# Work on the fifth tile of the next block between the two norms of a decoder trunk, in place of filler matmuls

## The chip, the cores and the metric

The kernel runs on one core of a Trainium2 chip. The metric is the device time of one execution in microseconds; the kernel before takes 794.01 us, the median of three runs (793.81 to 794.09).

## The reference

Two layers on 272 tokens (16 learned meta tokens and 256 of the sequence) of 1024 features, all in float32. Each layer is (cut):

```python
h = rms_norm(r, norm_mix_pre)
proj = h @ w_in        # q and kv latents, rotary key, diff q/k/v, two gates
...                    # latent attention and differential attention
mix = (sigmoid(g_a) * out_a + sigmoid(g_b) * out_b) @ w_out
r = r + rms_norm(mix, norm_mix_post)
h = rms_norm(r, norm_ffn_pre)
gu = h @ w_gate_up
ff = (silu(gu[..., :D_FF]) * gu[..., D_FF:]) @ w_down
r = r + rms_norm(ff, norm_ffn_post)
```

`rms_norm(x, gain)` is x / sqrt(mean(x*x) + 1e-6) * gain over all 1024 features. The result is r of the 256 tokens after layer 2.

## The kernel before

Features lie on the partitions and tokens on the free axis: r, y (the output of a block before its norm) and the block input h are 8 chunks of 128 features x 272 tokens; from the middle of layer 1 on only 256 tokens are needed. A float32 product is made of three matmuls in the rounded format float32r: each operand is split into a high and a low part, and w_hi·h_hi, w_hi·h_lo and w_lo·h_hi are added in PSUM (`block`, L1330 to L1332). A tile is 128 output features: 8 chunks x 3 matmuls for an input of 1024 features.

Weights come by DMA, 128x1024 at a time, to w_raw (4 buffers). ScalarE copies each to w_hi (L438) and VectorE subtracts to get w_lo (L883); both rings have 8 slots, and the splits run 6 to 7 slots ahead of TensorE. Each engine has its own written order of work; semaphores join them (`slot_ready` waits for a w_lo, `bank_free` and `emptied` for the evacuation of the tile that had the PSUM bank before, `pe_done` for a finished tile). VectorE empties the tiles in order and counts them in tile_free.

The three boundaries b = 1, 2, 3 are mix to gate/up in layer 0, down to the latents of layer 1, and mix to gate/up in layer 1. At each the block's last tile is squared, the squares (summed by GpSimd in acc) are summed over the features by TensorE (`norm_sums`, L1423), ScalarE takes the root (L485), VectorE the reciprocal (L891), and TensorE spreads it by transposes (`norm_spread`, L1442) into bank 7. VectorE then makes y·gain·rstd (L915) and adds it to r (L927) chunk by chunk, ScalarE makes h_hi (L492) and the next squares (L451), VectorE h_lo (L905). The norm of the next block isn't applied to h; its root is applied when its tiles are emptied (`rstd_h`), so its sums and spread stand inside the tiles that follow. Between its own norm steps TensorE multiplies an identity matrix into bank 6, 10 and 28 times (`keep_clock`, L1449, called by `post_norm`).

Then `first_tiles` (L1355, L1364) makes the first four tiles of the next block side by side, chunk by chunk, as h_hi and h_lo come. The fifth tile ("tile 4": `gu4`, or `lat 4` in layer 1) follows alone, with `norm_sums` of the next norm in front of chunk 0; in gate/up `norm_spread` stands in front of its chunk 4, in the latents it stands in `dq 1` in front of chunk 2. Gate/up tiles 0 to 5 use banks 0 to 5; tile 6 uses bank 2 again (it waits for the evacuation of tile 2), tile 7 bank 3, tile 8 bank 0, tile 9 bank 1, tile 10 bank 2. In gate/up VectorE copies rstd_h out of bank 7 (`take`, L896) and then goes pair by pair: evacuate (L1260), split (L883), evacuate, split, with the low part of the product (L1274) between. In the latents of layer 1, ScalarE squares and copies tile i (L451, L476), VectorE makes its low part (L974), with a split by each engine between; behind latent 4 come ScalarE's root (L485) and VectorE's reciprocal (L891).

During the gates of layer 0 VectorE computes the factors lambda (`lambdas`, L1000 to L1005), then the softmax of the meta tokens' rows (L1162 to L1175), whose result TensorE transposes inside gate tile 4 (`meta_transposes`, L1564).

Of the kernel before, what the change touches and what calls it, by code (L numbers as in the profile page):

```python
# [23 lines left out]
P = 128  # L24
D_MODEL, SEQ, DEPTH, N_META = 1024, 256, 2, 16
TOK = SEQ + N_META
# [17 lines left out]

TAIL = 8
# [141 lines left out]
def build_trunk(nc: bass.Bass, xT, x_rows, first_weights, weights, lam_in, consts, gain_rows, out):  # L187
# [4 lines left out]
    with ctx:  # L192
# [3 lines left out]
        def place(at, tensors):  # L196
# [16 lines left out]
            ("small", [P, 80], f32), ("pm_room", [P, 2, TOK], f32),  # L213
# [41 lines left out]

        (gain_bc, r_tok), _ = place(_, [("gain_bc", [P, D_MODEL], f32), ("r_tok", [P, 2, D_MODEL], f32)])
        assert _ <= nc.sbuf_usable_end
# [22 lines left out]
        gsub = small[:, 72:74]  # L280
        pscale, nscale = small[:, 32:35], small[:, 36:38]
# [25 lines left out]
        r_ready, h_hi, h_lo = sem("r_ready"), sem("h_hi_ready"), sem("h_lo_ready")  # L307
        lat_ready_hi = sem("lat_hi_ready")
# [55 lines left out]


        @block.sync
        def _(sp):
            def load(n, width, i=None, per=0):

                m = n if i is None else n + per * i  # L370
                if n >= FIRST + RAW:

                    sp.wait_ge(lo_ready, m - RAW + 1)
                src = weights[bass.ds(m * P, P), 0:width] if i is not None else weights[m * P:(m + 1) * P, 0:width]
                sp.dma_start(w_raw[:, n % RAW, 0:width], src).then_inc(raw_in[n % RAW], 16)


            for i, (a, b) in enumerate(PIECES):
# [33 lines left out]
            sp.wait_ge(pe_done, plan.tile_done[plan.tile[DEPTH - 1, "out", KC - 1]])  # L412
# [10 lines left out]
        def _(act):  # L423
# [44 lines left out]
            def latent(l, i):  # L468

                c0 = T0(l) if i < QC else 0  # L470
                t, K = plan.tile[l, "lat", i], NORMS * l + (NQ if i < QC else NKV)
                act.wait_ge(pe_done, plan.tile_done[t])
                if l and i == 0:
                    act.wait_ge(pt_ready, UNITS * l)
                square(K, i if i < QC else i - QC, ps[bank_of(t)][:, c0:TOK], c0)
                act.activation(lat_hi[:, i, c0:], ps[bank_of(t)][:, c0:TOK], ACT.Copy,  # L476
                               scale=gain[:, l, G_Q + i:G_Q + i + 1]).then_inc(lat_ready_hi, 1)
# [65 lines left out]
            for l in range(DEPTH):  # L543
# [194 lines left out]
                if l < DEPTH - 1:  # L738
                    for m in range(KC):
                        for j in range(4):  # L740
                            split(SD + 4 * m + j + HI_AHEAD)
                        square_tile(K0 + POST_FFN, TD + m, m)
                    root(K0 + POST_FFN, 7, D_MODEL, t0)
                    boundary(2 * l + 2, K0 + NORMS + PRE_MIX, G_MIXPRE, l + 1)
# [116 lines left out]
        def _(dve):  # L861
# [46 lines left out]
            def residual(b, K, gp, lp, t0):  # L908
# [3 lines left out]
                def product(c):  # L912
# [4 lines left out]
                    if c < KC - 1:  # L917
                        made[c] = step(ins)
                    else:
                        ins.then_inc(norm_ready, 1)  # L920

                def add(c):
                    if c < KC - 1:
                        after(made[c])
                    else:
                        dve.wait_ge(norm_ready, K + 1)
                    dve.tensor_tensor(r[:, c, t0:], r[:, c, t0:], parts[c % 2][:, t0:], ALU.add).then_inc(r_ready, 1)  # L927
# [9 lines left out]
                lo_part(b, KC - 2, *nxt(b), t0)  # L937
                lo_part(b, KC - 1, *nxt(b), t0)

            def nxt(b):  # L940
                return (G_FFNPRE, b // 2) if b % 2 else (G_MIXPRE, b // 2)
# [27 lines left out]
            def latent_lo(l, i):  # L969

                c0 = T0(l) if i < QC else 0
                t = plan.tile[l, "lat", i]
                dve.wait_ge(lat_ready_hi, 5 * l + i + 1)
                dve.scalar_tensor_tensor(out=lat_lo[:, i, c0:], in0=ps[bank_of(t)][:, c0:TOK], scalar=gain[:, l, G_Q + i:G_Q + i + 1],  # L974
# [21 lines left out]
            def lambdas():  # L996

                dve.wait_ge(lam_exp, 1)
                for l in range(DEPTH):
# [3 lines left out]
                    step(dve.tensor_scalar(gsub[:, l:l + 1], gain[:, l, G_SUB:G_SUB + 1], 1.0 - LAM_INIT[l], None, ALU.mult))  # L1003
                after(steps[0])
                dve.memset(idle, 0.0).then_inc(const_ready, 1)  # L1005

            for l in range(DEPTH):
# [239 lines left out]
                def pair(j, i=None, first=False):  # L1247
# [7 lines left out]
                    for k, buf in ((0, gbuf), (1, ubuf)):  # L1255
# [4 lines left out]
                        dve.tensor_tensor(buf[:, j % 2, t0:], ps[bank_of(t + k + (0 if i is None else RING))][:, t0:TOK], rstd_h[:, t0:], ALU.mult).then_inc(tile_free, 1)  # L1260
# [24 lines left out]
                if l < DEPTH - 1:  # L1285
                    for m in range(KC):
                        for j in range(4):
                            split(S("down") + 4 * m + j + AHEAD)
                        to_y(K0 + POST_FFN, TL("down") + m, m)
                    recip(K0 + POST_FFN, t0)  # L1290
# [25 lines left out]
        def _(pe):  # L1316
# [17 lines left out]
            def tile(t, n, at, width, src, t0, i=None, per=0, inside=None):  # L1334

                bank_free(t, i, per)
                for k, (a, b) in enumerate(src):
                    if inside and k in inside:
                        inside[k]()
                    mm = block(t, n, at + k * width, width, a, b, t0, k == 0, k == len(src) - 1, ahead=0 if i is None else per)  # L1340
                mm.then_inc(pe_done, 1)

# [121 lines left out]
            for l in range(DEPTH):  # L1464
# [13 lines left out]
                tile(TL("lat") + 4, S("lat") + 4, 0, P, full, 0, inside={0: lambda: norm_sums(K0 + PRE_MIX, 7, 0)} if l else None)  # L1478
# [231 lines left out]
                post_norm(K0 + POST_MIX)  # L1710
# [3 lines left out]
                for j in range(4, 4 + RING):  # L1714
                    slot_ready(g0 + j)
                    tile(gt + j, g0 + j, 0, P, late, t0, inside={0: lambda: norm_sums(K0 + PRE_FFN, 7, t0), 4: lambda: norm_spread(K0 + PRE_FFN, 7, t0)} if j == 4 else None)
# [20 lines left out]
                post_norm(K0 + POST_FFN)  # L1737
# [149 lines left out]
```

## Time and profile before

| | |
|---|---|
| median of three runs | 794.01 us |
| the profiled execution | 794.08 us |
| its span | 792.3 us |
| granted TensorE clock | 0.999 |
| TensorE busy | 785.0 us (99%), 6268 matmuls |
| VectorE busy | 572.3 us (72%) |
| ScalarE busy | 451.7 us (57%) |
| GpSimd busy | 138.6 us (17%) |
| bytes moved | 134.87 MB, mean 170 GB/s |

The span goes from the first to the last instruction that the profiler shows; the execution is 1.8 us longer. Busy of TensorE is an upper bound of its use, because matmuls are pipelined: one of 128x272 is shown with 0.29 us while the next starts 0.13 us later. PE is the matmul row, PEld the weight loads that overlap it. An idle time stands in brackets with the engine and the tensor that ended it. "issue" is idle time for which the profile shows no releaser.

### The profile page before, as it was taken

To read this page: it belongs to the slowest core of one execution; us is meant where nothing else is said; L and a number is where in the kernel's file an instruction comes from. 1 tells how busy PE (TensorE), PEld (TensorE's weight loads), DVE (VectorE), ACT (ScalarE), POOL (GpSimd) and SP (SyncE) were. 2 spreads that over 40 slices of the span, in tenths; PEclk is the share of its full clock that TensorE was granted. 3 is DMA by queue.
4 is the path that set the end of the run, shared out by engine and by line. 5 is a ranking of instruction groups with operands and counts; after the bars stand their busy time and mean duration, and the time that the engine had idled before them with its cause. 6 is when DMAs were issued, how large, how long until landed. Compare 5 with 4: busy or idle time off the path is not lost.

```text
span 792.3 us, 16792 instructions
## 1 busy us (share of the span) xinstructions
PE 785.0 (99%) x6268; PEld 762.2 (96%) x6268; DVE 572.3 (72%) x996; ACT 451.7 (57%) x766; POOL 138.6 (17%) x150
## 2 busy tenths in 40 slices
PE   9999999999999999999999999999999999999997
PEld 9999899999999999999999999999999999999885
DVE  6899787696787666766668987967866977676432
ACT  6657665675475454455557467656755755454331
POOL 0312000233321111101123302001433211111000
PEclk9999999999999999999999999999999999999999
DMA  9767433355166565355654674334552776667971
GB/s 334 255 225 241 131 109 107 107 187 160 55 206 218 161 176 172 115 166 170 198 173 134 192 241 153 107 108 132 187 167 73 227 215 178 195 175 193 276 135 54
DMA packets 55531, 134.87 MB, mean 170 GB/s; under 512 B 20896, under 2 KB 21536, under 8 KB 55344
## 3 DMA queue, kind: packets, MB, share of 16 engines
q1 hardware_dynamic: 38608, 131.43, 52.9%
q10 hardware_dynamic: 16864, 2.62, 2.0%
q8 instruction: 41, 0.67, 0.3%
q14 instruction: 18, 0.15, 0.1%
HBM read 131.93 MB, written 2.10 MB: 169 GB/s over the span
## 4 chain that ended last, share of the span: by engine, by line
PE 97%; DVE 1%; ACT 1%; issue 0%; DVEq 0%
PE bank L1330 24%; PE bank L1332 24%; PE bank L1331 24%; PE bank L1364 4%; PE bank L1748 3%; PE bank L1749 3%; PE bank L1747 3%; PE bank L1355 2%; PE bank L1602 2%; PE bank L1574 2%; PE bank L1621 1%; PE bank L1449 1%; PE bank L1423 1%; PE bank L1576 1%; PE bank L1380 1%; PE bank L1391 1%
## 5 line engine op out<-in xcount | busy, mean ns | idle before, releaser
L883 DVE TENSOR_TENSOR w_lo<-w_raw,w_hi 128x1024 fp32r<-128x1024 f32 x246 | 330.9, 1348 | 37.4 <-ACT w_hi L438 34.5
L1330 PE MATMUL bank<-h_hi,w_hi 128*128 128x272 f32 (+1 forms) x1200 | 346.0, 288 | 0.0
L1332 PE MATMUL bank<-h_hi,w_lo 128*128 128x272 f32 (+1 forms) x1200 | 342.8, 286 | 0.0
L1331 PE MATMUL bank<-h_lo,w_hi 128*128 128x272 f32 (+1 forms) x1200 | 341.9, 285 | 0.0
L438 ACT ACTIVATE w_hi<-w_raw 128x1024 fp32r<-128x1024 f32 x246 | 258.5, 1054 | 122.1 <-PE bank L1332 57.0
L1330 PEld LDWEIGHTS bank<-h_hi,w_hi 128*128 128x128 f32 x1200 | 226.2, 188 | 0.7
L1332 PEld LDWEIGHTS bank<-h_hi,w_lo 128*128 128x128 f32 x1200 | 226.2, 188 | 0.0
L1331 PEld LDWEIGHTS bank<-h_lo,w_hi 128*128 128x128 f32 x1200 | 226.0, 188 | 0.0
L848 POOL TENSOR_TENSOR pbuf<-sbuf,ubuf 128x272 f32<-128x272 f32 (+1 forms) x44 | 38.5, 874 | 205.6 <-DVE ubuf L1260 204.0
L779 POOL TENSOR_TENSOR acc<-acc,sq 128x272 f32<-128x272 f32 (+1 forms) x45 | 47.3, 1052 | 137.2 <-ACT sq L451 137.0
L1260 DVE TENSOR_TENSOR ubuf<-bank,rstd_h 128x272 f32<-128x272 f32 (+1 forms) x44 | 18.9, 430 | 44.9 <-PE bank L1332 44.9
L1330 PE MATMUL bank<-ff_hi,w_hi 128*128 128x272 f32 x176 | 50.7, 288 | 0.0
L1331 PE MATMUL bank<-ff_lo,w_hi 128*128 128x272 f32 x176 | 50.7, 288 | 0.0
L1332 PE MATMUL bank<-ff_hi,w_lo 128*128 128x272 f32 x176 | 50.5, 287 | 0.0
L721 ACT ACTIVATE sbuf<-gbuf 128x272 f32<-128x272 f32 (+1 forms) x44 | 18.7, 425 | 52.3 <-DVE gbuf L1260 52.2
L596 ACT ACTIVATE e_t<-e_t,small 128x272 f32<-128x272 f32 (+1 forms) x48 | 22.1, 462 | 44.9 <-DVE small L1115 44.9
L1748 PE MATMUL bank<-w_lo,ff_hi 128*128 128x512 f32 x88 | 34.7, 395 | 0.0
L1749 PE MATMUL bank<-w_hi,ff_lo 128*128 128x512 f32 x88 | 34.7, 394 | 0.0
L1747 PE MATMUL bank<-w_hi,ff_hi 128*128 128x512 f32 x88 | 34.6, 393 | 0.0
L1234 DVE COPY y<-bank 128x272 f32<-128x272 f32 (+1 forms) x24 | 10.4, 435 | 31.5 <-PE bank L1332 20.1
L1332 PEld LDWEIGHTS bank<-ff_hi,w_lo 128*128 128x128 f32 x176 | 33.1, 188 | 0.0
L1330 PEld LDWEIGHTS bank<-ff_hi,w_hi 128*128 128x128 f32 x176 | 33.1, 188 | 0.0
(238 smaller groups left out, 1229.2 us busy)
## 6 DMA issues: line engine op xcount, KB each, us to landing
w_raw<-weights SPq DMA_DIRECT2D x216, 512.0 KB, 3.9
w_raw<-weights SPq DMA_DIRECT2D x16, 384.0 KB, 3.2
w_raw<-weights SPq DMA_DIRECT2D x16, 320.0 KB, 2.9
w_first<-first_weights SPq DMA_DIRECT2D x2, 512.0 KB, 7.5
x_tok<-x_rows SPq DMA_DIRECT2D x1, 1024.0 KB, 11.0
turn<-y ACTq DMA_DIRECT2D x4, 256.0 KB, 7.1
r_tok<-turn ACTq DMA_DIRECT2D x8, 128.0 KB, 6.3
out_tokens<-o_tok SPq DMA_DIRECT2D x4, 256.0 KB, 2.0
```

The costliest lines, as they stand in the source:

```text
L438: act.activation(w_hi[:, n % RING, :], w_raw[:, n % RAW, :], ACT.Copy).then_inc(hi_ready, 1)
L596: last = act.activation(e[:, a:b], e[:, a:b], ACT.Exp, bias=mx[u % 2][:, s + part:s + part + 1], scale=-1.0, accum_out=sm[u % 2][:, s + pa ...
L779: pool.tensor_tensor(acc[:, K % 2, t0:], acc[:, K % 2, t0:], sq[:, plan.sq_place[K, c], t0:], ALU.add).then_inc(sq_added, 1)
L848: pool.tensor_tensor(pbuf[:, j % 2, t0:], sbuf_[:, j % 2, t0:], ubuf[:, j % 2, t0:], ALU.mult).then_inc(ff_prod, 1)
L883: dve.tensor_tensor(w_lo[:, n % RING, :], w_raw[:, n % RAW, :], w_hi[:, n % RING, :].bitcast(f32), ALU.subtract).then_inc(lo_ready, 1)
L1330: pe.matmul(dst, wh, hi, start=first, stop=False)
L1331: pe.matmul(dst, wh, lo, start=False, stop=False)
L1332: return pe.matmul(dst, wl, hi, start=False, stop=last)
L1364: pe.matmul(ps[bank_of(t)][:, t0:TOK], w[:, n % RING, k * P:(k + 1) * P], src[k][0], start=k == 0 and q == 0, stop=False)
L1747: pe.matmul(dst, x_hi, wh, start=k == 0, stop=False)
L1748: pe.matmul(dst, x_hi, wl, start=False, stop=False)
L1749: return pe.matmul(dst, x_lo, wh, start=False, stop=k == FC - 1)
```

## The change

At a boundary the next block's tile 4 is split by linearity. Its input is h = (r_old + y·g_post·rstd)·g_next, so w·h = w·(r_old·g_next) + rstd·[w·(y·g_post·g_next)]. For the first three of eight chunks (EARLY = 3) ScalarE and VectorE make high and low parts of r_old·g_next (old_hi, old_lo) and y·g_post·g_next (new_hi, new_lo) during the last tiles of the block, one part per tile. `post_norm` loses its fillers: TensorE multiplies the old parts into tile 4's bank and the new parts into bank 6. ScalarE copies bank 6 to new_part, VectorE multiplies that by the spread rstd, and when tile 4's other five chunks are done, VectorE adds tile and new_part; what read the tile's bank before now reads new_part. Nine products of two gains are made in `lambdas`. The sums of the next norm stand in front of chunk 3 of tile 4, the spread (gate/up) in front of chunk 7. The load of gain_bc, whose place overlaps new_part, waits for tile gu4 of the last layer instead of the last out tile. The diff, cut:

```diff
+EARLY = 3
...
 ScalarE
@@ latent(l, i)
+                src = ps[bank_of(t)][:, c0:TOK]
+                if l and i == 4:
+                    act.wait_ge(early_sum, 2 * l)
+                    src = new_part[:, c0:]
+                else:
+                    act.wait_ge(pe_done, plan.tile_done[t])
...
+            def early_high(b, i):
+                src, factor, hi, _ = early_chunk(b, i)
+                if b == 1 and i == EARLY:
+                    act.wait_ge(gains_ready, 1)
+                act.activation(hi, src, ACT.Copy, scale=factor).then_inc(early_hi, 1)
@@ boundary(b, K, g, l)
                 for c in range(KC):
+                    if c == 2:
+                        act.wait_ge(new_product, b)
+                        act.activation(new_part[:, t0:], ps[6][:, t0:TOK], ACT.Copy).then_inc(new_copied, 1)
@@ out tiles (down tiles of layer 0 likewise, with b = 2 l + 2)
                     square_tile(K0 + POST_MIX, TL("out") + m, m)
+                    if m < 2 * EARLY:
+                        early_high(2 * l + 1, m)
 VectorE
@@ residual(b, K, gp, lp, t0)
                 lo_part(b, KC - 2, *nxt(b), t0)
+                dve.wait_ge(new_copied, b)
+                dve.tensor_tensor(new_part[:, t0:], new_part[:, t0:], ps[7][:, 64 + t0:64 + TOK], ALU.mult).then_inc(norm_ready, 1)
                 lo_part(b, KC - 1, *nxt(b), t0)
...
+            def early_low(b, i):
+                src, factor, hi, lo = early_chunk(b, i)
+                dve.wait_ge(early_hi, 2 * EARLY * (b - 1) + i + 1)
+                dve.scalar_tensor_tensor(out=lo, in0=src, scalar=factor, in1=hi.bitcast(f32), op0=ALU.mult, op1=ALU.subtract).then_inc(early_lo, 1)
+            def early_tile(b, t):
+                t0 = boundary_from(b)
+                dve.wait_ge(pe_done, plan.tile_done[t])
+                dve.wait_ge(norm_ready, NORMS * ((b - 1) // 2) + (POST_MIX if b % 2 else POST_FFN) + 1)
+                dve.tensor_tensor(new_part[:, t0:], ps[bank_of(t)][:, t0:TOK], new_part[:, t0:], ALU.add).then_inc(early_sum, 1)
+                dve.wait_ge(early_sum, b)
@@ latent_lo(l, i)
+                if l and i == 4:
+                    early_tile(2 * l, t)
+                    src = new_part[:, c0:]
                 dve.wait_ge(lat_ready_hi, 5 * l + i + 1)
@@ lambdas()
+                for b in range(1, 2 * DEPTH):
+                    for c in range(EARLY):
+                        step(dve.tensor_tensor(both_gains[EARLY * (b - 1) + c], gain_before(b, c), gain_behind(b, c), ALU.mult))
                 after(steps[0])
@@ out tiles (down tiles likewise)
                     to_y(K0 + POST_MIX, TL("out") + m, m)
+                    if 1 <= m <= 2 * EARLY:
+                        early_low(2 * l + 1, m - 1)
@@ pair(j, i, first), gate/up
+                        if j == 2 and k == 0 and i is None:
+                            early_tile(2 * l + 1, t)
+                            src = new_part[:, t0:]
 TensorE
+            def early_old(t, n, c, t0):
+                dst = ps[bank_of(t)][:, t0:TOK]
+                wh, wl = (w[:, n % RING, c * P:(c + 1) * P] for w in (w_hi, w_lo))
+                pe.matmul(dst, wh, old_hi[:, c, t0:], start=c == 0, stop=False)
+                pe.matmul(dst, wl, old_hi[:, c, t0:], start=False, stop=False)
+                pe.matmul(dst, wh, old_lo[:, c, t0:], start=False, stop=False)
...
@@ post_norm
-            def post_norm(K):
+            def post_norm(K, b, t, n):
                 norm_sums(K, 7, t0)
-                keep_clock(10)
+                pe.wait_ge(early_lo, 2 * EARLY * b)
+                slot_ready(n)
+                bank_free(t)
+                early_old(t, n, 0, t0)
                 norm_spread(K, 7, t0)
-                keep_clock(28)
+                for c in range(1, EARLY):
+                    early_old(t, n, c, t0)
+                for c in range(EARLY):
+                    mm = early_new(n, c, t0)
+                mm.then_inc(new_product, 1)
@@ tile 4 of the latents of layer 1, and of gate/up
-                tile(TL("lat") + 4, S("lat") + 4, 0, P, full, 0, inside={0: lambda: norm_sums(K0 + PRE_MIX, 7, 0)} if l else None)
+                tile(TL("lat") + 4, S("lat") + 4, 0, P, full, 0, inside={EARLY: lambda: norm_sums(K0 + PRE_MIX, 7, 0)} if l else None, done=EARLY if l else 0)
...
+                        tile(gt + j, g0 + j, 0, P, late, t0, inside={EARLY: lambda: norm_sums(K0 + PRE_FFN, 7, t0), 7: lambda: norm_spread(K0 + PRE_FFN, 7, t0)}, done=EARLY)
```

`early_new` is `early_old` with new_hi, new_lo and bank 6. `tile(..., done=3)` skips the first three chunks and the wait for the bank.

## Rows read from the trace of the kernel before

**Rows 1.** The page, part 1: busy us (share of the span) and instructions of each engine.

```profile
PE 785.0 (99%) x6268; PEld 762.2 (96%) x6268; DVE 572.3 (72%) x996; ACT 451.7 (57%) x766; POOL 138.6 (17%) x150
```

**Rows 2.** Timeline, first boundary: start us, us, engine, line, operation, count, idle before.

```profile
203.70 0.30 PEld L1442 LDWEIGHTS bank<-cst,small 128*128 128x128 f32 x3 [0.16 <-DVE small L891]
...
203.97 1.66 PEld L1449 LDWEIGHTS bank<-identb 128*128 128x128 bf16 x28
...
205.29 0.52 ACT L492 ACTIVATE h_hi<-x_sb 128x272 fp32r<-128x272 f32 x1 [1.85 <-DVE x_sb L927]
...
205.92 0.19 PEld L1364 LDWEIGHTS bank<-h_hi,w_hi 128*128 128x128 f32 x1 [0.29 <-issue]
```

**Rows 3.** Timeline of PE in and behind tile gu4 of layer 0.

```profile
220.29 0.49 PE L1442 MATMUL bank<-cst,small 128*128 128x128 f32 x3
220.53 0.37 PE L1330 MATMUL bank<-h_hi,w_hi 128*128 128x272 f32 x1
...
220.99 0.29 PE L1330 MATMUL bank<-h_hi,w_hi 128*128 128x272 f32 x1
...
225.16 0.29 PE L1330 MATMUL bank<-h_hi,w_hi 128*128 128x272 f32 x1
```

**Rows 4.** Timeline of DVE behind the spread in gate/up of layer 0.

```profile
220.81 0.44 DVE L896 COPY rstd_h<-bank 128x272 f32<-128x272 f32 x1 [1.48 <-PE bank L1442]
...
224.32 0.43 DVE L1260 TENSOR_TENSOR gbuf<-bank,rstd_h 128x272 f32<-128x272 f32 x1
...
226.05 0.43 DVE L1260 TENSOR_TENSOR ubuf<-bank,rstd_h 128x272 f32<-128x272 f32 x1
```

**Rows 5.** Timeline around the start of tile gu6 of layer 1.

```profile
617.00 0.42 DVE L1260 TENSOR_TENSOR gbuf<-bank,rstd_h 128x256 f32<-128x256 f32 x1
...
617.33 0.19 PEld L1332 LDWEIGHTS bank<-h_hi,w_lo 128*128 128x128 f32 x1
...
617.53 0.19 PEld L1330 LDWEIGHTS bank<-h_hi,w_hi 128*128 128x128 f32 x1
```

**Rows 6.** Timeline of latent tile 4 of layer 1, until the spread.

```profile
427.94 1.21 DVE L883 TENSOR_TENSOR w_lo<-w_raw,w_hi 128x1024 fp32r<-128x1024 f32 x1
...
428.88 0.38 ACT L451 ACTIVATE sq<-bank 128x272 f32<-128x272 f32 x1
...
429.53 0.27 ACT L485 ACTIVATE small<-bank,small 128x3 f32<-128x3 f32 x1
...
429.68 0.50 DVE L974 SCALAR_TENSOR_TENSOR lat_lo<-bank,x_sb,lat_hi 128x272 fp32r<-128x272 f32 x1 [0.53 <-ACT lat_hi L476]
...
430.09 0.17 DVE L891 RECIPROCAL small<-small 128x3 f32<-128x3 f32 x1
...
431.15 0.34 PEld L1442 LDWEIGHTS bank<-cst,small 128*128 128x128 f32 x3
```

**Rows 7.** Timeline: lambdas and the next place at which DVE waits for PE, and PEld.

```profile
87.91 0.15 DVE L1002 TENSOR_SCALAR small<-small 128x1 f32<-128x1 f32 x1
87.98 0.14 DVE L1003 TENSOR_SCALAR small<-x_sb 128x1 f32<-128x1 f32 x1
88.04 0.15 DVE L1000 TENSOR_TENSOR small<-small 128x1 f32<-128x1 f32 x1
...
93.17 0.41 PEld L1564 LDWEIGHTS bank<-cst,pm 16*16 16x16 f32 x14 [0.30 <-DVE pm L1175]
...
106.84 0.44 DVE L901 TENSOR_TENSOR gates<-bank,rstd_h 128x272 f32<-128x272 f32 x1 [0.23 <-PE bank L1332]
```

**Rows 8.** Timeline: DVE at tile out 6 of layer 0; PEld at the third boundary's sums.

```profile
198.83 0.44 DVE L1234 COPY y<-bank 128x272 f32<-128x272 f32 x1 [1.46 <-PE bank L1332]
...
596.64 0.52 PEld L1423 LDWEIGHTS bank<-small,sq 128*128 128x128 f32 x4 [0.22 <-ACT sq L451]
```

**Rows 9.** Timeline of DVE: the reciprocal behind the first tiles, layer 0.

```profile
219.16 0.18 DVE L891 RECIPROCAL small<-small 128x3 f32<-128x3 f32 x1 [2.35 <-ACT small L485]
```

**Rows 10.** Windows, first boundary: busy us (PE, PEld, DVE, ACT, POOL), granted clock, DMA share, GB/s.

```profile
201.50:206.00 4.50, 4.35 (x57) 4.03 (x55) 2.27 (x6) 1.37 (x4) 0.00 (x0) 1.00 0.31 118
```

More of the change, by code:

```diff
@@ L212, in build_trunk @@
             ("cst", [P, C_ALL - 512 + 128], f32), ("identb", [P, P], bf16), ("maskb", [P, P], bf16),
-            ("small", [P, 80], f32), ("pm_room", [P, 2, TOK], f32),
+            ("small", [P, 88], f32), ("pm_room", [P, 2, TOK], f32),
             ("tres", [P, TOK], f32)])
@@ L254, in build_trunk @@
             ("ubuf", [P, 2, TOK], f32), ("sbuf", [P, 2, TOK], f32), ("pbuf", [P, 2, TOK], f32)])
+        (old_hi, old_lo, new_hi, new_lo, new_part), _end = place(att0 + 4 * 2 * FC * TOK, [
+            ("old_hi", [P, EARLY, TOK], f32r), ("old_lo", [P, EARLY, TOK], f32r), ("new_hi", [P, EARLY, TOK], f32r),
+            ("new_lo", [P, EARLY, TOK], f32r), ("new_part", [P, TOK], f32)])
         (gain_bc, r_tok), _ = place(_, [("gain_bc", [P, D_MODEL], f32), ("r_tok", [P, 2, D_MODEL], f32)])
-        assert _ <= nc.sbuf_usable_end
+        assert max(_, _end) <= nc.sbuf_usable_end
         (o_tok, o_sq), _ = place(base + 4 * ((RAW + 2 * RING) * SLOT + GAIN_COLS + KC * TOK), [("o_tok", [P, 2, D_MODEL], f32), ("o_sq", [P, 2, D_MODEL], f32)])
@@ L280, in build_trunk @@
         gsub = small[:, 72:74]
+        both_gains = [small[:, i:i + 1] for i in (*range(80, 88), 38)]
         pscale, nscale = small[:, 32:35], small[:, 36:38]
@@ L307, in build_trunk @@
         r_ready, h_hi, h_lo = sem("r_ready"), sem("h_hi_ready"), sem("h_lo_ready")
+        early_hi, early_lo, gains_ready, new_product, new_copied, early_sum = (
+            sem(n) for n in ("early_hi_ready", "early_lo_ready", "gains_ready", "new_product", "new_copied", "early_sum"))
         lat_ready_hi = sem("lat_hi_ready")
@@ L363, in boundary_from, with nxt, gain_before, gain_behind @@
             return N_META if b >= 2 * DEPTH - 1 else 0
+        def nxt(b):
+            return (G_FFNPRE, b // 2) if b % 2 else (G_MIXPRE, b // 2)
+        def gain_before(b, c):
+            l, g = (b - 1) // 2, G_MIXPOST if b % 2 else G_FFNPOST
+            return gain[:, l, g + c:g + c + 1]
+        def gain_behind(b, c):
+            g, l = nxt(b)
+            return gain[:, l, g + c:g + c + 1]
+        def early_chunk(b, i):
+            t0, c = boundary_from(b), i % EARLY
+            if i < EARLY:
+                return r[:, c, t0:], gain_behind(b, c), old_hi[:, c, t0:], old_lo[:, c, t0:]
+            return y[:, c, t0:], both_gains[EARLY * (b - 1) + c], new_hi[:, c, t0:], new_lo[:, c, t0:]
         @block.sync
@@ L410, in _ @@
                     first = d0 + 4 * KC
-            sp.wait_ge(pe_done, plan.tile_done[plan.tile[DEPTH - 1, "out", KC - 1]])
+            sp.wait_ge(pe_done, plan.tile_done[plan.tile[DEPTH - 1, "gu", 4]])
             sp.dma_start(gain_bc[:, :], gain_rows).then_inc(gain_rows_in, 16)
@@ L471, in latent @@
                 t, K = plan.tile[l, "lat", i], NORMS * l + (NQ if i < QC else NKV)
-                act.wait_ge(pe_done, plan.tile_done[t])
+                src = ps[bank_of(t)][:, c0:TOK]
[4 more added lines that the diff above has]
+                    act.wait_ge(pe_done, plan.tile_done[t])
                 if l and i == 0:
                     act.wait_ge(pt_ready, UNITS * l)
-                square(K, i if i < QC else i - QC, ps[bank_of(t)][:, c0:TOK], c0)
-                act.activation(lat_hi[:, i, c0:], ps[bank_of(t)][:, c0:TOK], ACT.Copy,
+                square(K, i if i < QC else i - QC, src, c0)
+                act.activation(lat_hi[:, i, c0:], src, ACT.Copy,
                                scale=gain[:, l, G_Q + i:G_Q + i + 1]).then_inc(lat_ready_hi, 1)
@@ L742, in _ @@
                         square_tile(K0 + POST_FFN, TD + m, m)
+                        if m < 2 * EARLY:
+                            early_high(2 * l + 2, m)
                     root(K0 + POST_FFN, 7, D_MODEL, t0)
@@ L916, in product @@
                                                    in1=ps[7][:, 64 + t0:64 + TOK], op0=ALU.mult, op1=ALU.mult)
[L917 to L920, printed above, removed]
+                    made[c] = step(ins)
                 def add(c):
[L923 to L926, printed above, removed]
+                    after(made[c])
                     dve.tensor_tensor(r[:, c, t0:], r[:, c, t0:], parts[c % 2][:, t0:], ALU.add).then_inc(r_ready, 1)
@@ L972, in latent_lo @@
                 t = plan.tile[l, "lat", i]
+                src = ps[bank_of(t)][:, c0:TOK]
+                if l and i == 4:
+                    early_tile(2 * l, t)
+                    src = new_part[:, c0:]
                 dve.wait_ge(lat_ready_hi, 5 * l + i + 1)
-                dve.scalar_tensor_tensor(out=lat_lo[:, i, c0:], in0=ps[bank_of(t)][:, c0:TOK], scalar=gain[:, l, G_Q + i:G_Q + i + 1],
+                dve.scalar_tensor_tensor(out=lat_lo[:, i, c0:], in0=src, scalar=gain[:, l, G_Q + i:G_Q + i + 1],
                                          in1=lat_hi[:, i, c0:].bitcast(f32), op0=ALU.mult, op1=ALU.subtract).then_inc(tile_free, 1)
@@ L1332, in block, with tile @@
                 return pe.matmul(dst, wl, hi, start=False, stop=last)
-            def tile(t, n, at, width, src, t0, i=None, per=0, inside=None):
-                bank_free(t, i, per)
+            def tile(t, n, at, width, src, t0, i=None, per=0, inside=None, done=0):
+                if not done:
+                    bank_free(t, i, per)
                 for k, (a, b) in enumerate(src):
+                    if k < done:
+                        continue
                     if inside and k in inside:
@@ L1341, in tile, with early_new @@
                 mm.then_inc(pe_done, 1)
+            def early_old(t, n, c, t0):
[4 more added lines that the diff above has]
+                pe.matmul(dst, wh, old_lo[:, c, t0:], start=False, stop=False)
+            def early_new(n, c, t0):
+                dst = ps[6][:, t0:TOK]
+                wh, wl = (w[:, n % RING, c * P:(c + 1) * P] for w in (w_hi, w_lo))
+                pe.matmul(dst, wh, new_hi[:, c, t0:], start=c == 0, stop=False)
+                pe.matmul(dst, wl, new_hi[:, c, t0:], start=False, stop=False)
+                return pe.matmul(dst, wh, new_lo[:, c, t0:], start=False, stop=c == EARLY - 1)
             def first_tiles(tiles, ready):
@@ L1715, in _ @@
                     slot_ready(g0 + j)
-                    tile(gt + j, g0 + j, 0, P, late, t0, inside={0: lambda: norm_sums(K0 + PRE_FFN, 7, t0), 4: lambda: norm_spread(K0 + PRE_FFN, 7, t0)} if j == 4 else None)
+                    if j == 4:
+                        tile(gt + j, g0 + j, 0, P, late, t0, inside={EARLY: lambda: norm_sums(K0 + PRE_FFN, 7, t0), 7: lambda: norm_spread(K0 + PRE_FFN, 7, t0)}, done=EARLY)
+                    else:
+                        tile(gt + j, g0 + j, 0, P, late, t0)
                 with pe.Fori(1, 5) as i:
@@ L1736, in _ @@
                         mm.then_inc(pe_done, 1)
-                post_norm(K0 + POST_FFN)
+                post_norm(K0 + POST_FFN, 2 * l + 2, plan.tile[l + 1, "lat", 4], plan.slot[l + 1, "lat", 4])
             d0 = S("down")
```

11 lines of the change are left out of this document (6 added, 5 removed).

## Prediction

> **What bounds the kernel now.** I read the page first: TensorE is busy 785.0 of 792.3 us, VectorE 72%, ScalarE 57% [rows 1]. Time can only be won by giving TensorE fewer real matmuls, or by filling a place where it does nothing of use. The chain of waits names such places: three times it leaves TensorE for the norm between two blocks. The timeline of the first one shows what happens there: the transposes that spread the reciprocal root load at 203.70, then 28 filler matmuls load from 203.97 for 1.66 us, VectorE and ScalarE make the first h_hi (to 205.81), and the first real weight load comes at 205.92 [rows 2]. So the fillers cover a latency of two other engines; TensorE arrives 0.29 us early. The change puts real work of the tile "number 4" of the next block there. Whether that is time won is decided by what TensorE meets next, so I followed each boundary on until TensorE next needs something from VectorE, and looked at the idle notes of PEld (a real stall shows there) and at VectorE's order.
>
> **The window itself.** In place of 28 fillers stand 2 old chunks and 3 new ones, 15 matmuls; the first old chunk (3) replaces the 10 fillers before the spread. A matmul of 128x272 takes its turn every 0.126 us: 33 of them lie between 220.99 and 225.16 [rows 3]. 15 x 0.126 = 1.90 us from 203.97 is 205.87, just in front of 205.92. The first ones behind transposes cost a little more: three in 0.46 us instead of 0.38 [rows 3]. So the first tiles begin 0 to 0.1 us later at each boundary; below nothing isn't possible, since they wait for the h_hi whose chain (sums, root, reciprocal, spread, product, add) isn't touched. I take 0.05 in all, bounds 0 to 0.3.
>
> **What leaves tile 4.** Nine matmuls, at each of three boundaries: 9 x 0.126 = 1.14 us, about 3.4 us in all (the third has 256 columns, so a little less). This is the gain if nothing else is late. At each boundary something is.
>
> *First boundary (gate/up, layer 0).* The sums now stand in front of chunk 3 and the spread in front of chunk 7: again 12 matmuls lie between them, so the spread stays at 220.29 and VectorE's copy of it at 220.81 [rows 3, 4]. From there VectorE runs without a pause: evacuate gu0, split, gu1, split, gu2 at 224.32 to 224.75 [rows 4]. Tile gu6 writes bank 2, which gu2 held. Before, TensorE came to gu6 at 225.16, 0.41 us after the bank was free. Now it arrives at 225.16 - 1.14 = 224.02 and waits for 224.75, plus 0.11 us from release to weight load (the third boundary shows such a restart: copy over at 617.42, load at 617.53 [rows 5]). It takes up at 224.86 instead of 225.16. The restart loses some overlap, so I take 0.2 us won, bounds 0.1 and 0.35. gu7 needs gu3, free at 226.48 [rows 4], and starts near 227.9: no second wait. VectorE's extra addition at gu4, 0.44 us by the row of an evacuation [rows 4], falls where it is behind but TensorE doesn't need it: the next bank from that queue is gu6's, four tiles on.
>
> *Third boundary (gate/up, layer 1).* Same order, but here TensorE already waits for that bank before the change: the weight load of gu6 comes at 617.53, 0.20 us after the one before it at 617.33, and gu2's evacuation ends at 617.42 [rows 5]. Arriving 1.1 us earlier wins nothing. I take 0, bounds 0 and 0.1.
>
> *Second boundary (latents of layer 1).* No bank is short, but the spread in dq1 waits for the reciprocal, and in front of that stand ScalarE's and VectorE's work on latent tile 4. Before: VectorE ends a split at 429.15, ScalarE squares at 428.88 and roots at 429.53, VectorE makes the low part at 429.68 and the reciprocal at 430.09 to 430.26; the spread loads at 431.15 [rows 6], so it has nearly a microsecond to spare. After: VectorE must first add new_part (0.44 us, as an evacuation), about 429.1 to 429.55, and only then can ScalarE square, 0.7 us later than before. Root, low part and reciprocal move with it, the reciprocal to about 430.95. TensorE comes to the spread at 431.15 - 1.14 = 430.01 and waits until about 431.0. Won: 0.15 us, bounds 0 and 0.5 (0.5 if the addition came a split earlier).
>
> **The setup.** lambdas() gets nine more multiplications of 128x1 and the end of the previous one is waited for. They stand in the middle of a VectorE run that TensorE waits for: it idles 0.30 us in front of meta_transposes until VectorE's pm, and VectorE has no wait for TensorE again until 106.84 [rows 7]. No cover there. Independent ones of these start 0.06 to 0.07 us apart (87.91, 87.98, 88.04 [rows 7]): 9 x 0.065 = 0.6 us, all of it on the path. From above: if each took its whole 0.15 us, 1.4 us; from below 0.5. I take 0.6, since the new ones are independent like the rows'. The Trainium skill, "VectorE: DVE Perf Modes", section Terms, says that a flush follows every operation and the next can't issue until the pipe is empty. By that the nine cost 1.4 us and the sum rises by 0.8; the trace disagrees, with starts 0.07 us apart for operations 0.15 us long.
>
> **The stages in front of the boundary.** ScalarE gets six copies (0.52 us each by h_hi's row [rows 2]) and VectorE six low parts (0.50 us [rows 6]), one a tile. VectorE idles 1.46 us in such a tile [rows 8], so both fit. Nearest to the edge is the third boundary: ScalarE's table load stands behind the sixth copy, the square of tile 6 and POOL's addition come about 0.4 us later and end near 595.9, where the first sums begin; but the second sums wait for the last square anyway, 0.22 us idle [rows 8]. Cost 0, bounds 0 and 0.1. During the first tiles VectorE's multiplication of new_part (0.44) meets an idle time of 2.35 us in front of the next reciprocal [rows 9]. On TensorE itself 18 matmuls in the window (3 in front of the spread, 15 behind) replace 9 in tile 4 and the 38 fillers.
>
> **Sum.** Span: + 0.6 (setup) + 0.05 (window) - 0.2 - 0.15 - 0 = + 0.3 us. The profiled run had 794.08 us, so 794.4; from the median, 794.01, it is 794.3. 0.2% of it is 1.6 us, about what a measurement of this kernel can tell from no change.
>
> **Rivals.**
> A. The nine matmuls are won at each boundary: - 3.4 + 0.6 = - 2.8, 791.2 us. For it: TensorE is 99% busy, and it does 27 matmuls fewer outside the windows. Against it: the bank of gu2 and the reciprocal, both with times that TensorE's arrival doesn't move. It would need VectorE to free gu2 by 224.0. Chance 0.08.
> B. Part of it: one of the two waits is shorter than I read, worth 0.6 to 1.1 us at one boundary, with the setup 0.6: 793.2 to 793.8 us; two of them make 792.4. Chance 0.1, nearly all within 0.2%.
> C. Slower: with the fillers gone, the pauses cost TensorE its clock. The place is the first tiles and gu6 (0.3 us before the spread, then about 0.85 us; also 1.0 us in dq1). The granted clock is 1.00 in the first boundary's stretch, where the longest pause is 0.29 us [rows 2, 10]; no pause of 1 us is there to read. At the level below, 1.2 GHz, a matmul takes its turn in 0.25 us, so each tile of 24 costs 3.0 us more. It decides from 11 matmuls at that level (1.4 us); one tile gives 797.3 us. The Trainium skill, "TensorE: Matmul & The Clock Gate", Part 1, has throttled as the default and activity as what releases it; by that rule the longer pauses are a risk and the dense real matmuls in the window none. Chance 0.04.
> D. The small operations cost their whole duration, or the window overruns at each boundary: 795.1 to 795.5 us. Chance 0.08, a fifth of it beyond 0.2% with the other bounds.
> My forecast holds 0.7. From these: faster by over 0.2% 0.09, within 0.85, slower 0.06. The range for eight in ten is 793.2 to 795.3: the bounds of the terms, and B and D at their near ends.
>
> **What would show it.** The profile after should have PEld idle of about 0.85 us at gu6 of layer 0, released by VectorE's gbuf, and about 1.0 us at gu6 of layer 1; an idle time of about 0.9 us at the spread in dq1, released by the reciprocal; 0.9 instead of 0.30 us in front of meta_transposes; first weight loads of the next block with 0.1 us or less idle; and no filler between 6 us and the end. The forecast is wrong if gu6 starts without idle time, if the gap between the reciprocal and the spread stays as wide as before in dq1, if the nine small operations cost nothing to the 93 us mark, or if the granted clock falls below 1.0 after a pause.

## The result, and the profile after

The changed kernel takes 795.3 us (median of 22 runs, 794.9 to 795.68) beside 794.03 us (22 runs, 793.64 to 794.71) of the kernel before on the same chip: a ratio of 1.0014, interval 1.0008 to 1.0020. That is within 0.2%, a little slower, and 1.0 us above the 794.3 forecast: the median lies on the upper bound of the range, 795.3. The profiled execution has a span of 793.8 us (792.3 before).

The page after, part 1 (busy us, share of the span, instructions of each engine):

```profile
PE 783.6 (99%) x6181; PEld 760.2 (96%) x6181; DVE 582.3 (73%) x1029; ACT 459.2 (58%) x787; POOL 143.1 (18%) x150
```

TensorE has 1.4 us less busy time than in [rows 1], and the span is 1.5 us longer: it now waits. The list of PEld's waits says where (line waited for: us in total, times, longest):

```profile
PEld bank L1528 <- DVE small L936: 2.1, 4, 1.2
PEld bank L1397 <- DVE w_lo L928: 2.0, 2, 1.1
PEld bank L1535 <- DVE identb L998: 1.1, 1, 1.1
PEld bank L1657 <- DVE pm L1234: 0.9, 1, 0.9
```

The third one stands before the first real matmul and was there before. The first was 0.3 us in all; it now has the 0.3 us in front of each boundary's spread and one wait of 1.16 us in dq1. The second is new, the fourth has grown. Now place by place; I line the two traces up by their matmuls and give TensorE's "offset", the start of a matmul after minus the start of the same one before. It is +0.3 us ahead of the setup.

*Setup.* VectorE's nine multiplications, and the load of `meta_transposes` behind them on PEld:

```profile
88.67 0.70 DVE L1062 TENSOR_TENSOR small<-x_sb 128x1 f32<-128x1 f32 x9
94.11 0.66 PEld L1657 LDWEIGHTS bank<-cst,pm 16*16 16x16 f32 x24 [0.95 <-DVE pm L1234]
```

Nine in 0.70 us from the first start to the last end, so some 0.07 us from start to start. The load comes at 94.11 and not 93.17 [rows 7], its idle time is 0.95 instead of 0.30, and the offset goes from 0.32 to 0.94.

*First boundary.* PEld, from the last sums to the first tiles:

```profile
203.84 0.19 PEld L1417 LDWEIGHTS bank<-old_hi,w_hi 128*128 128x128 f32 x1
...
204.57 0.30 PEld L1528 LDWEIGHTS bank<-cst,small 128*128 128x128 f32 x3 [0.30 <-DVE small L936]
204.84 0.19 PEld L1417 LDWEIGHTS bank<-old_hi,w_hi 128*128 128x128 f32 x1
...
206.58 0.19 PEld L1427 LDWEIGHTS bank<-new_lo,w_hi 128*128 128x128 f32 x1
206.80 0.19 PEld L1450 LDWEIGHTS bank<-h_hi,w_hi 128*128 128x128 f32 x1
```

Real matmuls stand where [rows 2] has fillers, and the first tile's load at 206.80 is the 205.92 of before plus the offset of 0.88: nothing won and nothing lost.

*gate/up tile gu6, layer 0.* VectorE's evacuation of gu2, then PEld and the first matmul:

```profile
225.18 0.43 DVE L1325 TENSOR_TENSOR gbuf<-bank,rstd_h 128x272 f32<-128x272 f32 x1
```

```profile
224.62 0.19 PEld L1399 LDWEIGHTS bank<-h_hi,w_lo 128*128 128x128 f32 x1
225.73 0.19 PEld L1397 LDWEIGHTS bank<-h_hi,w_hi 128*128 128x128 f32 x1 [0.92 <-DVE w_lo L928]
225.76 0.37 PE L1397 MATMUL bank<-h_hi,w_hi 128*128 128x272 f32 x1 [0.72 <-DVE gbuf L1325]
```

TensorE arrives 1.13 us sooner and then waits 0.92 us. Less the offset of 0.88, the evacuation starts at 224.30 [rows 4: 224.32] and the load at 224.85. The offset falls to 0.68: 0.2 us won. The two rows of this start disagree on the releaser: the load's names the split w_lo, the matmul's the evacuation, gbuf. The times speak for the evacuation: the load comes 0.12 us after its end at 225.61, while the next w_lo runs on to 226.96; experiment a_bank6 settles it.

*dq1, layer 1.* VectorE, then ScalarE, then PEld:

```profile
428.86 1.21 DVE L928 TENSOR_TENSOR w_lo<-w_raw,w_hi 128x1024 fp32r<-128x1024 f32 x1
430.00 0.43 DVE L992 TENSOR_TENSOR new_part<-bank,new_part 128x272 f32<-128x272 f32 x1
431.40 0.62 DVE L1030 SCALAR_TENSOR_TENSOR lat_lo<-new_part,x_sb,lat_hi 128x272 fp32r<-128x272 f32 x1 [0.98 <-ACT lat_hi L507]
431.94 0.16 DVE L936 RECIPROCAL small<-small 128x3 f32<-128x3 f32 x1
```

```profile
430.46 0.43 ACT L477 ACTIVATE sq<-new_part 128x272 f32<-128x272 f32 x1 [0.42 <-DVE new_part L992]
430.79 0.51 ACT L507 ACTIVATE lat_hi<-new_part,x_sb 128x272 fp32r<-128x272 f32 x1
431.20 0.24 ACT L516 ACTIVATE small<-bank,small 128x3 f32<-128x3 f32 x1
```

```profile
432.16 0.30 PEld L1528 LDWEIGHTS bank<-cst,small 128*128 128x128 f32 x3 [1.16 <-DVE small L936]
```

All of it hangs on the addition (new_part), which stands behind a split: square, high part, root, low part, reciprocal, in a row. TensorE had 9 matmuls fewer and waits 1.16 us. The offset is 0.94 ahead of tile 4 and 0.91 to 0.96 behind the spread: nothing won.

*gu6, layer 1.* VectorE's evacuation of gu2, and PEld:

```profile
618.17 0.42 DVE L1325 TENSOR_TENSOR gbuf<-bank,rstd_h 128x256 f32<-128x256 f32 x1
618.70 0.19 PEld L1397 LDWEIGHTS bank<-h_hi,w_hi 128*128 128x128 f32 x1 [1.07 <-DVE w_lo L928]
```

The load comes 0.11 us after the evacuation's end. 618.70 less the offset of 1.17 is 617.53, the same time as in [rows 5]. Nothing won.

*Between these places* the offset should stand still, and it does not. It falls by under 0.1 us over the attention of layer 0 and grows by 0.26 us over the 128x272 matmuls of the down projection of layer 0, by 0.2 over the attention and out tiles of layer 1, by 0.34 over the last stage. The first and the last 128x512 matmul of that last stage (264 of them), before and after:

```profile
725.53 0.40 PE L1747 MATMUL bank<-w_hi,ff_hi 128*128 128x512 f32 x1
...
786.48 0.39 PE L1749 MATMUL bank<-w_hi,ff_lo 128*128 128x512 f32 x1
```

```profile
726.71 0.40 PE L1843 MATMUL bank<-w_hi,ff_hi 128*128 128x512 f32 x1
...
787.99 0.40 PE L1845 MATMUL bank<-w_hi,ff_lo 128*128 128x512 f32 x1
```

60.95 us before and 61.28 after, with not one wait in it: every matmul takes its turn 1.3 ns later (0.2330 against 0.2318 us). No step of the prediction has this. The granted clock is 1.00 in all the stretches looked at, here at the first boundary and around the three long waits behind it (columns: us, PE busy, clock, DMA share, GB/s):

```profile
203.00:207.00 4.00, 3.92 (x31) 1.00 0.35 123
220.00:226.00 6.00, 5.28 (x43) 1.00 0.33 98
428.00:433.00 5.00, 4.04 (x35) 1.00 0.83 285
616.00:620.00 4.00, 3.10 (x27) 1.00 0.48 131
```

### The profile page after: what moved, and what is told of

Same layout as the page of the kernel before. It is cut to its first block, busy times and chain, and to the rows that moved or that the text cites. A ratio compares the mean times of both kernels' runs of the same rounds, so it can differ in the third digit from the quotient of the medians.

```text
span 793.8 us, 16676 instructions
## 1 busy us (share of the span) xinstructions
PE 783.6 (99%) x6181; PEld 760.2 (96%) x6181; DVE 582.3 (73%) x1029; ACT 459.2 (58%) x787; POOL 143.1 (18%) x150
## 4 chain that ended last, share of the span: by engine, by line
PE 95%; DVE 3%; ACT 1%; issue 1%; DVEq 0%; ACTq 0%
PE bank L1397 24%; PE bank L1398 23%; PE bank L1399 23%; PE bank L1450 4%; PE bank L1843 3%; PE bank L1845 3%; PE bank L1844 3%; PE bank L1441 2%; PE bank L1695 2%; PE bank L1667 2%; DVE w_lo L928 1%; PE bank L1714 1%; PE bank L1509 1%; PE bank L1669 1%; PE bank L1535 1%
## 5 line engine op out<-in xcount | busy, mean ns | idle before, releaser
L1397 PE MATMUL bank<-h_hi,w_hi 128*128 128x272 f32 (+1 forms) x1191 | 343.0, 288 | 1.6 <-DVE gbuf L1325 1.6
L1397 PEld LDWEIGHTS bank<-h_hi,w_hi 128*128 128x128 f32 x1191 | 224.6, 189 | 2.7 <-DVE w_lo L928 2.0
L824 POOL TENSOR_TENSOR acc<-acc,sq 128x272 f32<-128x272 f32 (+1 forms) x45 | 53.2, 1183 | 131.8 <-ACT sq L477 131.6
L1397 PE MATMUL bank<-ff_hi,w_hi 128*128 128x272 f32 x176 | 50.7, 288 | 0.0
L1397 PEld LDWEIGHTS bank<-ff_hi,w_hi 128*128 128x128 f32 x176 | 33.2, 188 | 0.0
L1398 PEld LDWEIGHTS bank<-ff_lo,w_hi 128*128 128x128 f32 x176 | 33.2, 188 | 0.0
```

Of the source, the lines that this page charges most:

```text
L824: pool.tensor_tensor(acc[:, K % 2, t0:], acc[:, K % 2, t0:], sq[:, plan.sq_place[K, c], t0:], ALU.add).then_inc(sq_added, 1)
L1397: pe.matmul(dst, wh, hi, start=first, stop=False)
L1398: pe.matmul(dst, wh, lo, start=False, stop=False)
```

## The experiments

b_small88, a_small80, a_gains and a_bank6 shared their runs of the kernel before (793.99 us), as did a_spread5, a_root, best and b_nofill (793.82), and b_b6root and b_no10, on another chip (793.98). The changed kernel was not run again beside them: what is said against it compares with the 795.3 us above, and the kernel before moved by up to 0.2 us between these groups. Offsets within the traces are given where that matters. All times are medians; the edits are shown cut.

**b_small88** and **a_small80: does the widened `small` slow the matmuls?** The change needs nine columns for its products and widened `small` from 80 to 88 columns, which moves every tensor laid out behind it by 32 bytes.

```
# b_small88, the kernel before
-  ("small", [P, 80], f32)
+  ("small", [P, 88], f32)
# a_small80, the changed kernel
-  ("small", [P, 88], f32)
+  ("small", [P, 80], f32)
-  both_gains = [small[:, i:i + 1] for i in (*range(80, 88), 38)]
+  both_gains = [... for i in (18, 19, 31, 35, 38, 39)] + [x_sb[:, i:i + 1] for i in (76, 77, 78)]
```

> The kernel before with one edit: the tensor of small constants has 88 columns instead of 80, nothing uses the 8 more. All tensors behind it lie 32 bytes further on, as in the changed kernel. Placement theory: matmuls that read ff_hi, ff_lo (and lat, am, od) change their pitch as they did in the changed kernel (ff 128x272 from 0.1249 to 0.1254 us, 128x512 from 0.2318 to 0.2330 us), 0.5 to 0.6 us in all: 794.6 us. Rival (the longer pitch comes from the extra copies, or is chance of one execution): no change, 794.0 us.

> The changed kernel with the nine products of gains in columns that were free, so that every older tensor lies where it lay before. Placement theory: 0.6 us less than the changed kernel, 794.7 us, with ff pitches as before. Rival: 795.3 us.

Measured: b_small88 794.62 us (794.26 to 795.24), ratio 1.0007 [0.9998, 1.0016]; a_small80 794.71 us (794.09 to 794.97), 1.0006 [0.9997, 1.0015]. The two ratios by themselves reach down to no change, so the traces decide. The first and last 128x512 matmul in b_small88, then in a_small80:

```profile
726.00 0.40 PE L1747 MATMUL bank<-w_hi,ff_hi 128*128 128x512 f32 x1
...
787.27 0.40 PE L1749 MATMUL bank<-w_hi,ff_lo 128*128 128x512 f32 x1
```

```profile
726.16 0.40 PE L1843 MATMUL bank<-w_hi,ff_hi 128*128 128x512 f32 x1
...
787.11 0.39 PE L1845 MATMUL bank<-w_hi,ff_lo 128*128 128x512 f32 x1
```

61.27 us and 60.95 us: the old kernel with the wide `small` has the slow turns, the new one with the narrow `small` the fast ones. Other shapes follow the width of `small` too, not all the same way (turn with 80 columns, then with 88): the down projection's 128x272 on ff 0.1249 and 0.1254 us; 128x256 on od, the differential attention's output, 0.1182 and 0.1188 in layer 1; 128x272 on od in layer 0 0.1259 and 0.1253. The 128x272 matmuls on h_hi and h_lo don't change, 0.1261. These turns go with the width in all twelve traces of this study, six of each. The placement is a cause of its own, worth 0.6 us. Which tensor's place matters, and why 32 bytes do, wasn't tried.

**a_gains: the setup.** The nine multiplications ahead of the wait for the lambdas' exponentials, in VectorE's idle time of 4.46 us:

```
  def lambdas():
+     (the nine tensor_tensor on both_gains)
      dve.wait_ge(lam_exp, 1)
      ...
-     (the nine)
```

> The changed kernel with the nine small multiplications in front of VectorE's wait for lam_exp (4.5 us idle there) instead of behind it. Theory: the idle time in front of meta_transposes goes back from 0.95 to 0.3 us and the kernel to 794.7 us. Rival (a later wait takes it back, since VectorE has slack elsewhere): 795.3 us.

Measured: 794.65 us (794.3 to 794.87), 1.0007 [0.9998, 1.0017]. Its PEld at the setup:

```profile
93.33 0.66 PEld L1657 LDWEIGHTS bank<-cst,pm 16*16 16x16 f32 x24 [0.33 <-DVE pm L1234]
```

The idle time is back at 0.33 us: 0.62 us won there, 0.65 in the median.

**a_bank6: the wait at gu6.** The accumulator has a further bank at that point; gu6 gets it instead of gu2's:

```
-  b = i if i < BANKS + EXTRA else i % BANKS
+  b = i if i < BANKS + EXTRA + 1 else i % BANKS
...
-  for b in range(BANKS, BANKS + EXTRA):        # banks to be emptied ahead of the next product
+  for b in range(BANKS, BANKS + EXTRA + 1):
```

> The changed kernel with gate/up tile 6 in bank 6 (free then) instead of bank 2, so it waits for no evacuation; VectorE's order is the same. Bank theory: the two idle times in front of gu6 (0.92 and 1.07 us) go, gu7 (arrival about 227.9) finds bank 3 free at 227.3: 1.9 us less than the changed kernel, 793.4 us. Rival, as the profile names the releaser (VectorE's w_lo split, so a weight slot isn't ready): both idle times stay, 795.3 us. Second rival: the wait moves on to gu7, less than 0.5 us won.

Measured: 793.2 us (792.72 to 793.51), 0.9986 [0.9977, 0.9995]: 2.1 us less than the changed kernel. In its list of PEld's waits L1397 is gone. The first two rows:

```profile
PEld bank L1528 <- DVE small L936: 2.1, 4, 1.2
PEld bank L1535 <- DVE identb L998: 1.1, 1, 1.1
```

The split that the load's row names as releaser is still there (225.37 to 226.82), and nothing waits for it: the wait was for the bank. By the offsets the two waits give back 2.0 us.

**a_spread5: can the evacuation come earlier?** The spread two chunks earlier in tile 4 (the expectation says tile 7 and two matmuls; it is gate/up tile 4 and six matmuls, as the edit shows):

```
-  7: lambda: norm_spread(K0 + PRE_FFN, 7, t0)
+  5: lambda: norm_spread(K0 + PRE_FFN, 7, t0)
```

> The changed kernel, but the spreading matmuls of the norm in front of the feed-forward part are put ahead of chunk 5 of gate/up tile 7's 8 chunks and not ahead of chunk 7 (two matmuls' room less). The first load behind them waited 0.92 us (layer 0) and 1.07 us (layer 1) for a bank of the accumulator. Theory (the wait is for the bank whose evacuation follows the norm, so an earlier spread lets VectorE reach the evacuation earlier): both waits shrink by 0.3 to 0.7 us, the time 793.8 to 794.7 us. Rival (the spread's inputs are not ready that early, so TensorE waits in front of the spread instead): no change or up to 0.5 us slower, 795.3 to 795.8 us.

Measured: 795.42 us (795.03 to 795.82), 1.0018 [1.0009, 1.0027]: nothing won. The theory fell. The rival's time came, but not its reason: in front of the spread the waits are those of the changed kernel. VectorE in this kernel:

```profile
222.67 0.43 DVE L1325 TENSOR_TENSOR ubuf<-bank,rstd_h 128x272 f32<-128x272 f32 x1
223.45 1.65 DVE L928 TENSOR_TENSOR w_lo<-w_raw,w_hi 128x1024 fp32r<-128x1024 f32 x1 [0.35 <-ACT w_hi L464]
225.03 0.43 DVE L1325 TENSOR_TENSOR gbuf<-bank,rstd_h 128x272 f32<-128x272 f32 x1
```

The evacuation of gu1 does come a microsecond earlier (223.64 in the changed kernel). But the split between it and gu2's then waits 0.35 us for ScalarE's high part and lasts 1.65 us instead of 1.23. So gu2's evacuation stays where it was (less the offsets, 224.38 us here and 224.31 in the changed kernel), and TensorE waits 0.97 us. VectorE's queue has two limits that lie close together. Why the split lasts longer isn't shown.

**a_root: the wait in dq1.** Root and reciprocal are queued behind latent tile 3, so that the late addition doesn't hold them up:

```
# ScalarE
-  if l and i == 4:
+  if l and i == 3:
       root(K0 + PRE_MIX, 7, D_MODEL, 0)
+  if l and i == 4:
       latent_eps(K0 + PRE_MIX)
# VectorE
   latent_lo(l, i)
+  if i == 3:
+      recip(K0 + PRE_MIX, 0)
```

> The changed kernel, but ScalarE's root and VectorE's reciprocal of the norm ahead of the latent projection's next layer are queued behind latent tile 3 and no longer behind latent tile 4. In the changed kernel TensorE idles 1.16 us in front of that norm's three spreading matmuls, which end a chain new_part (VectorE) - square (ScalarE) - sums - root - reciprocal; the root, at 431.20, and the reciprocal, at 431.94, run late in it. Theory (the queue position of root and reciprocal holds TensorE up): the idle falls to about 0.2 us, the time from 795.3 to 794.2 us. Rival (the sums, not the queue, decide: the reciprocal can't run earlier, or the stall moves to the next unit): no change, 795.0 to 795.5 us.

Measured: 794.11 us (793.68 to 794.45), 1.0003 [0.9994, 1.0012], 1.2 us less than the changed kernel; by the offsets 1.1 us. The reciprocal and the spread:

```profile
428.38 0.16 DVE L937 RECIPROCAL small<-small 128x3 f32<-128x3 f32 x1
```

```profile
430.44 0.34 PEld L1530 LDWEIGHTS bank<-cst,small 128*128 128x128 f32 x3
```

No idle time is left in front of it. The sums had been ready: the root's place in the queue was what held it up.

**best: the four edits together** (a_small80, a_gains, a_bank6, a_root).

> Four single edits of the changed kernel in one: the nine products of gains in free columns, so that no tensor moves (-0.6 us by its own run), those products ahead of the wait for the lambdas (-0.65), gate/up tile 6 in an accumulator bank of its own (-2.1), root and reciprocal of the latent norm one tile earlier (-1.1 expected, not yet run alone). If the four add up: 795.3 - 4.4 = 790.9 us, about 3 us below the kernel before. Rival (the gaps share a cover, so that closing one opens the next): 791.8 to 792.6 us.

Measured: 790.55 us (790.32 to 790.93, 5 runs), ratio 0.9961 [0.9948, 0.9975]: 3.3 us faster than the kernel before. Single gains of 0.6, 0.65, 2.1 and 1.2 us make 4.55, and 4.75 came; by the offsets from the setup on, 4.4 and 4.5. They add up. This is rival A's mechanism at last: against the kernel before, the offset falls by 1.14, 1.14 and 1.06 us at the three boundaries, the nine matmuls of each. Waits of PEld, the first rows; the long ones are gone, and the 0.3 us in front of each spread remain:

```profile
PEld bank L1537 <- DVE identb L999: 1.1, 1, 1.1
PEld bank L1530 <- DVE small L937: 0.9, 3, 0.3
```

**b_b6root: does that gain belong to the change?** The bank and the root edit on the kernel before.

> The kernel before with two of the four edits that brought the changed kernel to 790.55 us: gate/up tile 6 in an accumulator bank of its own, and root and reciprocal of the latent norm behind latent tile 3. (The other two, on the nine products, have no counterpart in it.) It asks how much of the 3.3 us below the kernel before belongs to the moved matmuls. Theory (the two edits only remove waits that the moved matmuls uncovered; 27 matmuls at 0.126 us are the 3.3 us): 793.6 to 794.2 us, no change. Rival (the two edits are worth time by themselves): 792.5 us or less.

Measured: 793.82 us (793.46 to 794.13), 0.9998 [0.9989, 1.0007]. They are worth nothing there: they only let through what the moved matmuls bring, 27 at 0.118 to 0.126 us, 3.3 us.

**b_nofill and b_no10: what were the fillers for?** Rival C asked whether the pauses cost TensorE its clock.

```
   norm_sums(K, 7, t0)
-  keep_clock(10)          # out in both
   norm_spread(K, 7, t0)
-  keep_clock(28)          # out in b_nofill only
```

> The kernel before without the filler matmuls (10 and 28 at each of the three boundaries), whose results nobody reads: TensorE waits idle for the norm there. Theory one (pauses of this length cost no clock; the changed kernel idled up to 1.16 us at a granted clock of 1.00): no change, 794.0 us, within 0.3. Theory two (the fillers hold the clock up, the changed kernel lost nothing only because its matmuls took their place): the granted clock shows below 1.00 behind a boundary, and each of the three costs at least 1.5 us, 798 us or more.

Measured: 799.67 us (797.87 to 799.91, 6 runs), 1.0067 [1.0055, 1.0079]. Windows of it at the first boundary (columns as above):

```profile
203.00:206.00 3.00, 0.74 (x5) 0.76 0.18 70
206.00:210.00 4.00, 3.98 (x17) 0.50 0.00 0
210.00:220.00 10.00, 10.00 (x76) 0.93 0.17 50
```

and its pauses on PEld:

```profile
203.76 0.30 PEld L1442 LDWEIGHTS bank<-cst,small 128*128 128x128 f32 x3 [0.65 <-DVE small L891]
205.99 0.29 PEld L1364 LDWEIGHTS bank<-h_hi,w_hi 128*128 128x128 f32 x1 [1.93 <-issue]
```

Theory two holds. The granted clock stands at 0.50, the 1.2 GHz level, where matmuls of 128x272 start 0.227 us apart (206.38, 206.61, 206.84) and not 0.126, and the first tiles pay: by the offsets 2.4, 1.5 and 1.5 us at the three boundaries.

> The kernel before without the 10 filler matmuls between the sums and the spread of each boundary; the 28 behind the spread stay. Without both, TensorE idled 0.65 us and, behind three matmuls, 1.93 us, and the granted clock then stood at 0.50 for about 5 us; the kernel took 799.7 us. Theory (the long pause brings the clock down, a pause like the short one, or the 1.1 us ones of the changed kernel, does not): clock 1.00 everywhere, 793.8 to 794.3 us. Rival (the short pause is enough): the clock falls behind each boundary, 796 us or more.

Measured: 794.57 us (12 runs), 1.0012 [1.0002, 1.0021], but spread over 793.51 to 796.97. Seven lie at 794.62 or below with a mean clock of 0.998 or more, two near 795.5 with 0.997, three at 796.8 to 797.0 with 0.994. My theory was half wrong. In the profiled execution the pause at the first boundary was enough (PEld, then windows):

```profile
203.88 0.30 PEld L1442 LDWEIGHTS bank<-cst,small 128*128 128x128 f32 x3 [0.65 <-DVE small L891]
204.15 2.61 PEld L1449 LDWEIGHTS bank<-identb 128*128 128x128 bf16 x28
```

```profile
203.00:204.00 1.00, 0.44 (x4) 1.00 0.56 225
204.00:205.00 1.00, 1.00 (x14) 0.85 0.00 0
205.00:206.00 1.00, 1.00 (x13) 0.50 0.00 0
208.00:209.00 1.00, 1.00 (x10) 0.94 0.05 16
```

The clock fell, the 28 fillers took 2.61 us and not 1.66 [rows 2], and 1.3 us were lost. At the other two boundaries of the same execution the pauses were 0.65 and 0.64 us, the 28 fillers took 1.66, and nothing was lost. So such a pause, behind the narrow matmuls of the sums, brings the clock down at times. The changed kernel has three real matmuls in that place, 0.30 us of idle time, and none of its 22 runs shows a mean clock below 0.998. Its waits of 0.92 to 1.16 us stand behind dense real matmuls, and the clock stayed at 1.00 there.

## Why the prediction was near, and what it lacked

- **Setup, + 0.6.** Right: 0.62 by the offset, 0.65 by a_gains. The starts 0.07 us apart hold for the nine.
- **Window, + 0.05.** Right within its bounds: no change at any boundary that the offsets show. Rival C, slower by the clock, did not come. b_nofill and b_no10 show that an emptied window can cost the clock; in the changed kernel the moved matmuls fill it. The long pauses that rival C also named, at gu6 and in dq1, did not touch the clock. Its price was too high: at the lower level a matmul took its turn in 0.227 us and not 0.25, so a tile of 24 costs 2.4 us more and not 3.0.
- **gu6 of layer 0, - 0.2.** Right, in each part: evacuation, restart (0.12 us) and load within 0.02 us of the forecast times. **gu6 of layer 1, 0.** Right: 617.53, as forecast. a_bank6 shows the cause, and the price of both waits: 2.1 us.
- **dq1, - 0.15.** The mechanism was right and the size off by 0.2. The addition started at 429.06 (430.00 less the offset of 0.94), where I had about 429.1. I then moved the reciprocal's end by the same 0.7 us as the square, to 430.95; it ended at 431.16. The low part in front of it started 0.8 us later than before and took 0.62 us instead of 0.50. The load follows at 431.22; I had let TensorE go on at 431.0. Nothing was won. What I had not seen is that root and reciprocal needed only another place in their queues for this wait to go.
- **Stages in front, 0.** No wait appeared there in the trace after.
- **The missing term, + 0.6.** "The setup" counted the nine products' time and not their columns. The diff widens `small`, and what lies behind it moves. b_small88 gives this alone; a_small80 takes it back. With it, and with 0 instead of - 0.15 in dq1, the sum is + 1.05 in place of + 0.3. The medians say + 1.3. From the setup to the end the offset grows by 1.2 us, and there the terms come within 0.1 us of it: 0.62 at the setup, 0.7 by the placement (0.26, 0.2 and 0.34 less the 0.1 of layer 0's attention), - 0.2 at gu6. The rest is within what medians of this kernel vary by. The two spans differ by 1.5 us; of that + 0.3 had gathered before the setup, in code that doesn't differ, where other kernels of this study show - 0.4 to + 0.3 of the same.
- **The range** held by luck. Its upper bound, 795.3, came from other terms' bounds and from rival D; nothing in it stood for the placement, and the median fell on it.
- **Rival A** was right about the worth of the matmuls and wrong about this kernel. In the trace after, 27 matmuls fewer in the tiles are 3.3 us, and 0.92 + 1.16 + 1.07 = 3.15 us of it went into new waits. best gets them back.

## What to carry to other kernels

When matmuls are moved out of a busy stretch into a pause, follow TensorE from there to the next thing it needs from another engine; what it gains before that is only lent, and the repair is then often a matter of one bank or one place in a queue. A releaser that the profile names is worth checking against its end time, and against the row of the matmul behind the load: here the load came 0.12 us after the end of another instruction, which the matmul's row named. An edit that widens a buffer can shift the pace of matmuls that it doesn't touch, so compare the pitch of unchanged matmuls between two traces before looking for waits.

## What the runs showed of the hardware that was not expected

- Moving tensors by 32 bytes changed the pace of matmuls that read them: 128x512 from 0.2318 to 0.2330 us, 128x272 of the down projection from 0.1249 to 0.1254 us, and, in the other direction, 128x272 of layer 0's attention from 0.1259 to 0.1253 us. It came and went with the width of `small` in twelve kernels, six of each width; b_small88 changes nothing else.
- A pause of 0.65 us behind narrow matmuls was followed by a granted clock of 0.50 at one boundary, and pauses of 0.65 and 0.64 us by 1.00 at the other two of the same execution (b_no10). Pauses of 0.92 to 1.16 us behind dense real matmuls left it at 1.00.
